# A hybrid decoder layer on eight cores: six of sixteen x tiles read feature-major instead of transposed on TensorE

## The reference, cut to what matters

```python
h    = rmsnorm(x, norm_pre)                 # per token: x * rsqrt(mean(x*x)+eps) * gain per feature
proj = einsum('bsd,de->bse', h, w_in)       # [xA | gA | u | v | gB | q | gC], 7168 columns
ya = pool_mixer(xa, w_pool, scale) * silu(ga)
yb = (u * (tril(w_s) @ layernorm(v) + b)) * silu(gb)   # per chunk of 128 tokens, 8 heads
yc = memory_cross_attention(q, k_m, v_m) * silu(gc)    # 4 heads, softmax over 256 memory tokens
y  = concat(rmsnorm(ya), rmsnorm(yb), rmsnorm(yc))
x  = x + rmsnorm(y @ w_out, norm_post)
```

## Time and profile before

| | |
|---|---|
| median of 3 runs | 1244.76 us (1244.74 to 1244.83) |
| the profiled execution's own time | 1244.6 us |
| its span (core 5, the slowest) | 1243.0 us |
| spans of the eight cores | 1240.2 to 1243.0 us |
| TensorE clock granted, mean | 0.997 (the 2.4 GHz level) |
| TensorE busy | 1215.4 us (98%) |
| VectorE, ScalarE, GpSimd busy | 493.8, 465.2, 216.2 us |

### The profile page before, as it was taken

The page is one execution under the profiler, slowest core; times in us unless marked ns, Lnnn a source line. Parts: engine busy times, 40 slices in busy tenths (PEclk is TensorE's granted clock), DMA queues, the critical chain, the costliest instruction groups (busy, mean ns, idle before and its releaser), DMA issues.

```text
span 1243.0 us, 17870 instructions; the slowest of 8 cores (1240.2 to 1243.0 us)
## 1 busy us (share of the span) xinstructions
PE 1215.4 (98%) x6248; PEld 583.3 (47%) x6248; DVE 493.8 (40%) x788; ACT 465.2 (37%) x863; POOL 216.2 (17%) x206
## 2 busy tenths in 40 slices
PE   5989999999999999999999999999999999999997
PEld 3445444444444455554554444444444444444443
DVE  5477533323223333444443233333332544343434
ACT  4277633422222332231225555555632232222222
POOL 1000001121221011211121101211232222222222
PEclk9999999999999999999999999999999999999998
DMA  8976513652425362635535541452795583543332
GB/s 222 221 186 160 108 48 76 114 98 57 71 53 90 72 111 43 105 82 95 96 63 96 86 84 31 81 86 67 168 205 135 167 274 98 158 147 106 96 108 68
DMA packets 50937, 137.82 MB, mean 111 GB/s; under 512 B 22785, under 2 KB 35201, under 8 KB 37137
## 3 DMA queue, kind: packets, MB, share of 16 engines
q0 software_dynamic: 7632, 50.86, 25.7%
q1 hardware_dynamic: 43218, 85.83, 24.0%
HBM read 153.39 MB, written 29.36 MB: 147 GB/s over the span
## 4 chain that ended last, share of the span: by engine, by line
PE 94%; DVE 2%; ACT 1%; DMA 1%; issue 1%; DVEq 0%; SPq 0%; ACTq 0%
PE ps L280 93%; PE ps L283 1%; DMA mem_pages<-x 1%; DVE mem_pages L400 1%; ACT mem_pages L394 0%; ACT mem_pages L1067 0%; ACT L1067 0%; DVE stat L1062 0%; DVE mem_pages L1072 0%; DVE stat L560 0%; ACT stat L257 0%; SPq L292 0%; DVE mem_pages L1193 0%; DVE mem_pages L785 0%; ACT mem_pages L516 0%
## 5 line engine op out<-in xcount | busy, mean ns | idle before, releaser
L280 PE MATMUL ps<-mem_pages 128*128 128x512 bf16 (+2 forms) x5784 | 1191.2, 368 | 4.2 <-ACT mem_pages L414 1.9
L280 PEld LDWEIGHTS ps<-mem_pages 128*128 128x128 bf16 x5784 | 557.3, 98 | 621.3 <-issue 13.1
L750 POOL TENSOR_TENSOR mem_pages<-mem_pages 128x512 f32<-128x512 f32 x72 | 91.1, 1266 | 600.3 <-ACT mem_pages L743 598.0
L737 ACT ACTIVATE mem_pages<-mem_pages,small_c 128x512 bf16<-128x512 f32 x96 | 68.8, 716 | 276.1 <-DVE mem_pages L809 148.5
L1167 DVE SCALAR_TENSOR_TENSOR mem_pages<-ps,stat,mem_pages 128x512 f32<-128x512 f32 (+1 forms) x130 | 96.5, 742 | 161.1 <-PE ps L280 135.4
L1175 POOL TENSOR_TENSOR mem_pages<-mem_pages 128x512 f32<-128x512 f32 (+1 forms) x65 | 81.3, 1251 | 249.8 <-ACT jk L1171 249.8
L1171 ACT ACTIVATE jk<-mem_pages 128x512 bf16<-128x512 f32 (+1 forms) x65 | 40.5, 623 | 214.4 <-DVE mem_pages L1167 214.4
L940 DVE TENSOR_TENSOR mem_pages<-mem_pages 128x526 f32<-128x526 f32 (+3 forms) x80 | 56.1, 702 | 101.3 <-ACT mem_pages L934 96.2
L799 DVE TENSOR_TENSOR mem_pages<-ps,mem_pages 128x512 f32<-128x512 f32 x32 | 22.1, 691 | 141.0 <-PE ps L280 141.0
L785 DVE CAST mem_pages<-ps 128x512 bf16<-128x512 f32 (+1 forms) x24 | 14.4, 602 | 124.3 <-PE ps L280 121.1
L769 ACT ACTIVATE mem_pages<-ps 128x512 f32<-128x512 f32 x96 | 54.5, 591 | 22.2 <-PE ps L280 18.8
(11 more groups left out here) (61 smaller groups left out, 430.9 us busy)
## 6 DMA issues: line engine op xcount, KB each, us to landing
mem_pages<-w_pages POOLq DMA_DIRECT2D x44, 1024.0 KB, 13.1
mem_pages<-x SPq DMA_DIRECT2D x32, 1024.0 KB, 9.3
out<-mem_pages SPq DMA_DIRECT2D x15, 1024.0 KB, 6.3
y_scr<-mem_pages SPq DMA_DIRECT2D x96, 128.0 KB, 2.3
mem_pages<-y_scr SPq DMA_DIRECT2D x12, 1024.0 KB, 13.5
mem_pages<-w_pages POOLq DMA_DIRECT2D x8, 512.0 KB, 20.4
mem_pages<-mem SPq DMA_DIRECT2D x2, 1024.0 KB, 6.8
mem_pages<-mem_norm SPq DMA_DIRECT2D x1, 1024.0 KB
```

The source lines that it names most:

```text
L280: return lambda e: e.matmul(out, lhsT=lhsT, rhs=rhs, start=start, stop=stop)
L737: P.op("act", lambda e: e.activation(out=yv, in_=tmp, func=AF.Copy, scale=gbr[:, c:c + 1]), reads=[tmp_b[i], gbr_b], writes=[ring_b[r]])
L750: P.op("pool", lambda e: e.tensor_tensor(out=accl_v if last else acc, in0=acc, in1=dst, op=ALU.add), reads=[dst_b, acc_b[tb]], writes=[acc ...
```

## The change

- The host adds a second copy of tiles 9 and 11 to 15 of x, `xf`, in which each tile has features on the partitions (16 blocks of 128 features, each with 128 tokens in a row). The gain comes as 16 more columns of `small`.
- `fm_load` reads such a tile on SP into one of two f32 pages, and POOL multiplies it by the gain in place. `fm_rstd` still squares and sums the ordinary tile on ACT and forms 1/rms, issues the next ordinary load (`x_load(i+4)`), then stores the 128 values to `r_scr` in device memory and, once that store has landed, reads them back as a row on all partitions (`rstd_rows`). `fm_norm` multiplies by that row on DVE straight into `hT`. These six tiles have no transposes and no copies out of PSUM.
- The scratch for `sgu_load` moves to page `VN[3]`, and it is issued after the load of tile 11; the page list now gives pages 20 and 21 to `xf`, so `pump` issues no weight in tile 7, and `gb` 0, `u` 0, `gb` 1 in tiles 13, 14, 15, into pages 20, 21 and 9.
- `c_1a_copy(1)` stands ahead of `c_1b(0)`.
- The last tile's sum: four partial sums and eps are added on DVE between the last unit's two DVE steps (`slsum`); ACT then takes the root with the fifth as input and the sum as bias.

```diff
+FM_TILES = (9, 11, 12, 13, 14, 15)
...
+    def fm_load(i):
+        n = FM_TILES.index(i)
+        s = n % 2
...
+        dma_sp(xf, xf_d[n * 128:(n + 1) * 128, :], writes=[fm_b[s]], sem="d_xf%d" % s)
+        xv = xf.rearrange("p (k t) -> p k t", k=16)
+        P.op("pool", lambda e: e.tensor_tensor(out=xv, in0=xv, in1=g, op=ALU.mult),
+             reads=[fm_b[s], small_b], writes=[fm_b[s]])
+
+    def fm_rstd(i):
+        s = FM_TILES.index(i) % 2
+        x_a(i, (1,))
+        stb = st_x[ST_SSX + i]
+        rstd_of(sc(ST_SSX + i), sc(ST_SSX + i), stb)
+        x_load(i + 4)
+        tok = dma_sp(r_d[i].rearrange("(p o) -> p o", o=1), sc(ST_SSX + i), reads=[stb], sem="d_rs%d" % s)
+        dma_sp(rrow[:, s * 128:(s + 1) * 128], r_d[i].partition_broadcast(128), writes=[rrow_b[s]],
+               sem="d_rr%d" % s, waits=[tok])
+
+    def fm_norm(i):
...
+        P.op("dve", lambda e: e.tensor_tensor(out=dst, in0=xv, in1=rv, op=ALU.mult),
+             reads=[fm_b[s], rrow_b[s]], writes=hT_b[i])
+        if n + 2 >= len(FM_TILES):
+            drop(fm_p[s])
+        else:
+            fm_load(FM_TILES[n + 2])
...
+    x_load(8)
+    x_load(9)
     for tt in range(4, NTT):
...
-        if tt + 1 < NTT:
+        if tt + 1 < NTT and tt + 1 not in FM_TILES:
             x_pe(tt + 1)
         if tt == 4:
             x_a(6, (2,))
+            x_load(10)
+            fm_load(FM_TILES[0])
...
-        elif tt + 2 <= NTT:
+        elif tt + 2 <= NTT and tt + 2 not in FM_TILES:
             x_a(tt + 2)
+            x_load(tt + 6)
...
         v_mm(tt, 1, 1)
+        if tt + 3 in FM_TILES:
+            fm_rstd(tt + 3)
+        if tt + 2 in FM_TILES:
+            fm_norm(tt + 2)
         v_ln(tt)
-        if tt + 4 <= NTT:
-            x_load(tt + 4)
+        if tt == 5:
+            sgu_load()
+            fm_load(FM_TILES[1])
+        if tt == 7:
+            sgu_mask()
...
-            pump(1, waits=[xt_b[3].wtok])
-            pump(1)
...
     c_1a(1)
+    c_1a_copy(1)
     c_1b(0)
-    c_1a_copy(1)
...
-            wo_unit(tt, 3, 256, 256, ST_SL + 4)
+            wo_unit(tt, 3, 256, 256, ST_SL + 5, slsum)
```

More of the change, by code:

```diff
@@ L170, in build_program @@
     sgu_b_d = din("sgu_b", [1024])
-    small_d = din("small", [128, 112])
+    small_d = din("small", [128, 128])
     ident_d = din("c_ident", [128, 128], BF16)
@@ L185, in build_program @@
     oss = sb("oss", [128, 8], BF16)
-    small = sb("small_c", [128, 112], F32)
+    small = sb("small_c", [128, 128], F32)
+    rrow = sb("rstd_rows", [128, 256], F32)
     accl = sb("accl", [128, 1024], BF16)
@@ L609, in build_program @@
     take(*VN)
-    vn_b += [nbuf("vn%d" % tt, VN[tt // 4]) for tt in range(NTT)]
+    vn_b += [nbuf("vn%d" % tt, VN[tt // 4]) for tt in range(12)]
     for part in range(2):
@@ L649, in sgu_mask @@
                                               op=ALU.mult), reads=wt["b"], writes=[wsT_b])
-        drop(p)
+        drop(p, dyn=False)
+        take(p)
+        vn_b.extend([nbuf("vn%d" % tt, p) for tt in range(12, NTT)])
     def sgu_bias(half, b):
@@ L1145, in load_xres, with slsum, wo_unit @@
         xres[tt] = (p, b)
-    def wo_unit(tt, db, lo=0, n=512, so=None):
+    def slsum():
+        t = NTT - 1
+        P.op("dve", lambda e: e.reduce_sum(out=sc(ST_FO + t), in_=stat[:, ST_SL:ST_SL + 5], axis=AX.X),
+             reads=[so_b[t], stat_b], writes=[sl_b])
+    def wo_unit(tt, db, lo=0, n=512, so=None, mid=None):
         tb = tt // 4
@@ L1166, in wo_unit @@
         for br in (1, 2):
+            if br == 2 and mid is not None:
+                mid()
             P.op("dve", lambda e, br=br: e.scalar_tensor_tensor(
@@ L1182, in wo_final @@
         stf = Buf("stf")
-        c0, cn = (ST_SL, 5) if last else (ST_SO + tt * 4, 4)
-        P.op("dve", lambda e: e.reduce_sum(out=sc(ST_FO + tt), in_=stat[:, c0:c0 + cn], axis=AX.X),
-             reads=[so_b[tt]], writes=[stf])
-        rstd_of(sc(ST_FR + tt), sc(ST_FO + tt), stf)
+        if last:
+            P.op("act", lambda e: e.activation(out=sc(ST_FR + tt), in_=sc(ST_SL + 5), func=AF.Sqrt,
+                                               bias=sc(ST_FO + tt)), reads=[so_b[tt], sl_b], writes=[stf])
+            P.op("dve", lambda e: e.reciprocal(out=sc(ST_FR + tt), in_=sc(ST_FR + tt)), reads=[stf], writes=[stf])
+        else:
+            P.op("dve", lambda e: e.reduce_sum(out=sc(ST_FO + tt), in_=stat[:, ST_SO + tt * 4:ST_SO + tt * 4 + 4],
+                                               axis=AX.X), reads=[so_b[tt]], writes=[stf])
+            rstd_of(sc(ST_FR + tt), sc(ST_FO + tt), stf)
         xp, xb = xres[tt]
@@ L1354 @@
         m["mem"] = mem[b]
-        m["small"] = f(np.concatenate([cols, _cinv(half)], axis=1))
+        m["small"] = f(np.concatenate([cols, _cinv(half), gcol], axis=1))
+        xs = m["x"].reshape(NTT, 128, 16, 128)[list(FM_TILES)]
+        m["xf"] = f(xs.transpose(0, 3, 2, 1).reshape(len(FM_TILES) * 128, D))
         m.update(_consts())
```

29 lines of the change are left out of this document (21 added, 8 removed).

## The result

| | before | after |
|---|---|---|
| median | 1244.88 us (6 runs, 1244.74 to 1245.44) | 1357.88 us (6 runs, 1336.59 to 1490.12) |
| ratio, 95% interval | | 1.080 (1.0756 to 1.0844), slower |
| profiled execution, its span | 1244.6, 1243.0 us | 1359.0, 1357.5 us |

Four of the six executions after the change were disturbed by a lower clock on some cores; the ratio rests on the other two, 1336.59 and 1352.44 us. By them the change costs about 100 us. Forecast were 17.6 us (1262.2, range 1247 to 1268): the sign was right, the size far off. Unless another core is named, rows are of the slowest core of the profiled execution.

What follows compares the result with a forecast made beforehand. TensorE, 98% busy, was taken to bound the kernel. Loop end +11.3 us (transposes included), weights +7.6, small edits -1.0 and -0.3 gave +17.6 on 1244.6: 1262.2 us, slower, range 1247 to 1268.

Steps and rivals of the forecast that it cites:

- Transposes: TensorE in the v loop: six tiles lose 16 transposes each, 6 x 0.89 us, -5.3 us.
- The first row of 1/rms: At tile 9 in the v loop: the row comes late behind a backlog of loads, leaving TensorE idle for 12.4 us.
- step 2: SP's queue at tile 9: the small store lands when everything ahead of it is through, with nothing added for itself.
- Step 1: At tile 9: after ACT's sum of squares and DVE's reciprocal, SP can store the 128 values at about 85.6.
- Rival E: POOL's 4.4 us products make DVE's two-input products wait, 2.5 us in each of three buffer rounds: 1270; chance 0.05.
- Step 3: SP's queue at tile 9: the backlog of sgu loads and tiles ends at 100.7; the row is read back by 103.2.
- The rest of the loop: V loop after tile 9: row 11 2.1 us late and 2 us for buffer rounds at tiles 13 to 15, +4.0 us.
- Weights: Behind the v loop: gb 0 1.0 us late and u 0 6.6 us late, together +7.6 us.
- Small edits: Query copies ahead of the first softmax, -1.0 us; ACT's root in the tail no longer behind its last accumulation, -0.3 us.
- Rival B: The small store gets through beside the bulk, so every row and the weights are in time: 1238.0 us, faster; chance 0.11.

Runs made afterwards that it cites:

- e_pe: The change with the row of 1/rms spread by a VectorE diagonal and one matmul instead of through device memory: 1250.37 us, ratio 1.004.
- e_nostore: The change without the store of 1/rms and its wait, the row being read from the gain: 1260.08 us, ratio 1.0104.
- e_apart: The change with the 128 stored values 512 B apart; the read-back still waits but fetches a row of the gain: 1264.84 us, ratio 1.016.
- e_nowait: The change with the store still made, but the row read from the gain without waiting for it: 1284.59 us, ratio 1.0319.
- e_small: The kernel before with only the two small edits, query copies ahead of the first softmax and the last sum split: 1243.9 us, ratio 0.9994.
- e_best: e_split with sgu's operands read ahead of tile 10 and the row's matmul behind the tile's own: ratio 0.9982; median of all twelve executions 1268.2 us.
- e_split: e_pe with POOL's product by the gain cut into eight pieces: 1266.93 us, ratio 1.0179.
- e_probe: The kernel before with six extra small transfers on SP's queue between the B blocks, results unused: 1245.5 us.
- e_probe3: The kernel before with extra small stores on SP's queue only where no weight page is in flight: 1245.6 us.

## Why the prediction was right in sign and wrong in size

- **Transposes, -5.3 us:** right as far as the count goes; TensorE has 96 instructions fewer (6152 against 6248), six times 16. "In the v loop it runs without a gap" holds only from 78 us on: gaps of 1.57, 0.28 and 1.40 stand ahead of it, before and after.
- **The first row of 1/rms, step 2, is the one that failed.** "For 128 values of 4 bytes I therefore take the time until all ahead of it is through, plus nothing." The measured price of such a store is 13.7 us on a quiet queue and 15.5 to 21.2 in the change, a term missing at each of six tiles. The nearest rows were stores in pieces of a kilobyte and a load, and I took them for bytes where the price is by small values and their spacing. So the term for the store itself was put at nothing, without a row that showed it. I had drawn the upper bound from the queue alone. The range should have held a price for an operation of which the trace had no row.
- **Step 1, the store issued at 85.6:** it came at 89.67. 3.3 us of the 4.1 are the 128x1 VectorE instruction held by POOL's product. Rival E was right in its mechanism. POOL's product takes 3.6 us where the prediction had 4.4, and what it holds varies by core and kernel: here an instruction that the prediction did not name (0.16 us became 3.46), in e_pe the scaling (2.35 became 5.40), in e_nostore the product by the row (2.29 became 4.07). "Against it" was no evidence, as means of groups that seldom run together can't show it.
- **Step 3, the backlog:** right. In the change the DMA engines fell idle at 100, forecast 100.7. With the store's own price gone the store landed at 102.3 (e_apart), and the backlog alone gave a gap of 8.15 (e_nostore).
- **The rest of the loop, +4.0 us:** 56.5 us in five gaps. The reckoning by buffer rounds was right in kind and is 3.4 us in e_apart (0.26 + 0.21 + 1.92 + 1.05); in the change each later row paid the store's price again.
- **What a pending store does to others** was not in the sum: some 25 us without any wait for it (e_nowait against e_nostore).
- **The clock** was not in the sum: about 2 us a gap, some 12 us on core 0, and on some cores a stretch at 0.81 that costs some 25 us more.
- **Weights, +7.6 us:** hidden in the change, since the loop ended later than they landed; 3.02 in e_apart, so over-sized by more than half.
- **Small edits, -1.0 and -0.3 us:** -0.8 measured, within the noise; the wait at the softmax is gone (e_small), and the tail's -0.3 was not read by itself.
- **Rival B, faster at 1238.0:** false for this kernel. Without the route through device memory something near it exists: e_best at 1240.7 to 1243.5, and single cores of it at 1235, when the clock holds.

Still open: what brings the stretches at 0.81. They need no pause that the undisturbed cores don't have as well (e_split), nor do they come with every dense stretch (e_small has none in eleven executions). I tried nothing that separates this. Nor is it shown by which step of the DMA engine neighbouring values become slow, and at which distance exactly that ends; reading, modifying and writing one piece of memory in turn would fit, but no run tests it.

## What to carry to other kernels

Price a small store by how many small pieces lie close together in device memory, and by what else is in flight, not by its bytes alone; a column of 128 values laid side by side was the dearest half kilobyte measured here, and a row that all partitions need was cheaper through one matmul (e_pe, 1250.4 us). Where a step has no row in the trace, measure it alone in the old kernel before building on it: here one extra DMA in the kernel before took 21.4 us (e_probe). And count what a pending transfer or a long GpSimd instruction does to those that merely stand beside it.

## What the runs showed of the hardware that was not expected

- 128 values of 4 bytes: 13.7 us side by side, 8.8 us 8 B apart, 2.9 us 32 B apart, 2.2 us 512 B apart; side by side with weight pages in flight, 21.4 and 22.6.
- A slow store delays the completion of what is issued behind it on its queue: from 6.4 to 14.8 us and from 2.1 to 7.9 (e_probe), and on a quiet queue from 2.3 to 7.1, the moment at which the slow one landed (e_probe3).
- POOL's 128x2048 product holds a VectorE instruction of 0.16 us for 3.46 us, even where that one reads a single column.
- A single gap of 32 us costs 2.6 us more than its length. Cores that pause no more than the others can lose more, in neighbouring pairs: a clock of 0.81 from about 85 to 240 us ends them some 28 us later (e_split).
